# Three edits around the modulation rows of a two-layer S5 and attention trunk

## The chip, the cores and the metric

The kernel runs on one core of one Trainium2 chip. The metric is the device time of one execution in microseconds (us), the median of three runs; smaller is better. A core has a matrix engine (PE, with its weight loads listed apart as PEld), VectorE (DVE), ScalarE (ACT), GpSimd (POOL) and SyncE (SP), each with an instruction stream of its own, which wait for each other on semaphores. DMAs are issued from the streams of SP and ACT here.

## The reference, cut to what matters

Everything is fp32. The sequence has 512 positions of 1024 features, batch 1.

```python
cond = silu(c)
for i in range(2):
    mod = cond @ ada_w[i] + ada_b[i]                    # (1, 6 * 1024)
    sh_t, sc_t, g_t, sh_c, sc_c, g_c = split(mod, 6)
    h = rms_norm(x, norm_g[i, 0]) * (1 + sc_t) + sh_t
    h = s5_mixer(h, ...) if i == 0 else diff_attention(h, ...)
    x = x + g_t * rms_norm(h, norm_g[i, 1])
    h = rms_norm(x, norm_g[i, 2]) * (1 + sc_c) + sh_c
    h = conv_ffn(h, w_in[i], conv_w[i], conv_b[i], w_out[i])
    x = x + g_c * rms_norm(h, norm_g[i, 3])
```

`s5_mixer` ends in a gated product (GLU) with a 1024 x 2048 matrix. `conv_ffn` is an up projection (1024 x 5632), a causal convolution of width 3 along the sequence, `gelu(a) * b`, and a down projection (2816 x 1024).

## The kernel before, in words

All large products run in "units" of weights of 128 x 2048 fp32 (1 MB). SP loads unit `n` into `raw[:, n % 2]`, ACT copies it rounded into `whi` (`split_high`, L783), DVE writes the remainder into `wlo` (`split_low`, L1388), and PE multiplies: each step is three matmuls (hi x hi, lo x hi, hi x lo), 48 matmuls in a unit. One half (slot) of `raw`, `whi` and `wlo` is filled while PE works from the other. SP loads unit `n` once unit `n - 2` has been split (`load_unit`). The stages are the S5 front (Toeplitz tiles `toep`, loaded by 32 DMAs of SP from `kx`, one set of eight for each of four pieces), 8 GLU units, `barrier(0)` (root mean squares, and the hidden input of the next product, made feature tile by feature tile in `next_input` on DVE and `high` on ACT), 22 up units and 12 down units of the first FFN, attention, and a second FFN of the same form.

The modulation of layer 0 and 1 is 2 x 48 x 128 numbers, worked out in six "thirds" of 2048. Each third arises as four rows of 512 in one PSUM bank, on partitions 0, 32, 64 and 96. For layer 0 (thirds 0 to 2) PE makes the rows itself in the S5 front (`ada_unit`, L1867). For layer 1 (thirds 3 to 5) DVE adds up products in `ada_acc` (`ada_step`, L1453), and PE sums over the partitions (`sum_acc`, L1885, eight matmul records). ACT copies the bank into `sq` (`copy_row`, L721; `copy_sums`, L935), and PE turns it by eight matmul records against columns of the identity (`turn_row`, L1879) into 16 columns of bank 7. There DVE reads it in `modulation` (L1307 on) and adds the bias into `modt`.

In the order of the streams: `turn_row(1)` and `turn_row(2)` stand between GLU unit 0 (L2077) and GLU unit 1 (L2043 on). In the first FFN PE runs `sum_acc(0)` after up unit 1, `turn_row(3)` and `sum_acc(1)` after unit 9, `turn_row(4)` and `sum_acc(2)` after unit 13, `turn_row(5)` after unit 15. `barrier(0)` makes `row_of(5)` (L2155) when POOL's first root is there, four idle products (L2116), `row_of(7)` when POOL's second root is there, six idle products, and then the up units begin on the first `hhi` tile (L2051).

For an up unit, ACT's `body` copies the two banks with the last tap into `ca` and `cb` (L925), splits the unit after next (L783), applies gelu (L929), and after POOL's product (L609) writes `ghi` (L931); DVE's `body` does the other taps (L1584, L1588) and then `split_low`; POOL writes `glo` (L611). Down unit 0 has only half the work (24 matmuls), since the first half of its rows is padding; its weights are split in the body of up unit 20, those of down unit 1 in the body of up unit 21, the last.

On ACT `copy_row(1)` stands among the scaling of the S5 input (`scaled`, L740), and `copy_row(2)` just after it, ahead of `z_steps` (L790), `zt_steps` (L800) and the split of the first GLU unit.

Of the kernel before, what the change touches and what calls it, by code (L numbers as in the profile page):

```python
# [24 lines left out]
P = 128  # L25
# [51 lines left out]
def build(nc, a, out_rows):  # L77

    ctx = ExitStack()
    with ctx:  # L80
# [129 lines left out]
        psum = ctx.enter_context(nc.psum_tensor("psum", [P, 8, 512], F32))  # L210

# [40 lines left out]
        acc_psum = sem("acc_psum")  # L252
        turned_x, rows_out = sem("turned_x"), sem("rows_out")
# [418 lines left out]
        def _(act):  # L672
# [49 lines left out]

            def copy_inputs(g, beside=None):

                for n in range(4):
                    act.wait_ge(inb_psum, 4 * g + n + 1)
                    gp = PO * g + 4 * (n % 2)
                    A((inb_im if n // 2 else inb_re)[:, gp:gp + 4, :],
                      psum[:, n % 2, :].rearrange("p (g k) -> p g k", g=4), ACT.Copy).then_inc(inb_ready, 1)
                    if beside:  # L730
                        beside(n)
# [32 lines left out]
            copy_row(1)  # L764
            scaled(1, 3)
# [36 lines left out]

            copy_row(2)
            z_steps(0)
            z_steps(1)
            zt_steps(0)
            act.wait_ge(in_psum, 2)
# [66 lines left out]
            def copy_gate_row(hf, bank):  # L874

                act.wait_ge(mod_psum, 6 + hf)
                A(gate_row[:, SEQ * hf:SEQ * hf + SEQ], psum[:, bank, :], ACT.Copy).then_inc(row_copied, 1)
# [28 lines left out]

            def high(r):

                layer, c0 = shift_col(r)
                for f in range(KT):  # L910
                    act.wait_ge(t_ready, KT * r + f + 1)
                    A(hhi[:, f, :], psum[:, 4 + 2 * (f % 2), :], ACT.Identity,
                      bias=modt[:, layer, c0 + f:c0 + f + 1]).then_inc(h_hi, 1)
                    if r == 2 and f == 1:
                        copy_gate_row(1, 3)

            def ffn(layer):
                n0, g0 = U_FIN[layer], layer * JT

                def body(j, s, half):  # L920
# [6 lines left out]
                    split_high(j + (n0 + 2), s, half + n0 // 2 + 1)  # L927
# [5 lines left out]
                def copy_sums(third):  # L933
                    act.wait_ge(acc_psum, third - 2)
                    A(sq[:, third % 2, :], psum[:, 6, :], ACT.Copy).then_inc(row_copied, 1)  # L935

                body(0, 0, 0)
                body(1, 1, 0)
                if layer == 0:
                    copy_sums(3)  # L940
                    pairs(act, 2, 10, body)
                    copy_sums(4)
                    pairs(act, 10, 14, body)
                    copy_sums(5)
                    pairs(act, 14, JT, body)
                else:
                    pairs(act, 2, JT, body)
# [19 lines left out]
            second_half_high()  # L967
            high(0)
# [154 lines left out]
        def _(dve):  # L1123
# [179 lines left out]
            def modulation(layer, chunks):  # L1303

                for ch in chunks:
                    c = slice(KT * ch, KT * ch + KT)
                    link(TT(modt[:, layer, c], psum[:, 7, 48 * layer + KT * ch:48 * layer + KT * ch + KT],  # L1307
                            ada_b[:, layer, c], ALU.add))
# [269 lines left out]
            def ffn(layer):  # L1578
                n0, g0 = U_FIN[layer], layer * JT

                def body(j, s, half, first=None, second=None):
# [10 lines left out]
                    split_low(j + (n0 + 2), s, half)  # L1592
# [3 lines left out]
                if layer == 0:  # L1596
# [9 lines left out]
                    pairs(dve, 12, 16, body)  # L1606
                    dve.wait_ge(mod_psum, 5)
# [4 lines left out]
                    pairs(dve, 16, JT, body)  # L1612
                else:
                    pairs(dve, 0, JT, body)
# [48 lines left out]
            def glu(i, s):  # L1663
# [193 lines left out]
        def _(pe):  # L1857
# [16 lines left out]
            def turn_row(third):  # L1874

                pe.wait_ge(row_copied, third + 1)
                for q in range(4):
                    out = psum[:, 7, THIRD * third:THIRD * third + THIRD].rearrange("p (b q) -> p q b", q=4)
# [3 lines left out]
            def sum_acc(third, slot):  # L1882

                for b in range(4):
                    ins = M(psum[32 * b:32 * b + 1, 6, :], ones[:, 0:1], ada_acc[:, slot, 512 * b:512 * b + 512],  # L1885
# [38 lines left out]
            turn_row(0)  # L1924
# [175 lines left out]
            turn_row(1)  # L2100
            turn_row(2)
# [57 lines left out]
            def barrier(r):  # L2159
# [30 lines left out]
                if r == 2:  # L2190
                    broadcast_gate(0, 2)
                else:
# [53 lines left out]
            def ffn(layer):  # L2246
# [348 lines left out]
```

## Time and profile before

| | |
|---|---|
| median of three runs (lowest, highest) | 1226.2 us (1224.52, 1226.31) |
| profiled execution, its time and its span | 1226.44 us, 1224.6 us |
| PE busy | 1191.5 us, 97% |
| DVE, ACT, POOL busy | 739.4, 519.1, 398.6 us |
| mean granted clock of PE, as a share of full speed | 0.996 |
| DMA packets, all queues | 26696 |

A row of the profile gives the start or count, the length and the line of `kernel.py`; "idle before" is the time its engine had nothing to do, with the engine that released it. Matmul records overlap: back to back the up units' matmuls are 0.39 us long each and start 0.23 us apart.

### The profile page before, as it was taken

To read this page: it belongs to the slowest core of one execution; us is meant where nothing else is said; L and a number is where in the kernel's file an instruction comes from. 1 tells how busy PE (TensorE), PEld (TensorE's weight loads), DVE (VectorE), ACT (ScalarE), POOL (GpSimd) and SP (SyncE) were. 2 spreads that over 40 slices of the span, in tenths; PEclk is the share of its full clock that TensorE was granted. 3 is DMA by queue.
4 is the path that set the end of the run, shared out by engine and by line. 5 is a ranking of instruction groups with operands and counts; after the bars stand their busy time and mean duration, and the time that the engine had idled before them with its cause. 6 is when DMAs were issued, how large, how long until landed. Compare 5 with 4: busy or idle time off the path is not lost.

```text
span 1224.6 us, 17448 instructions
## 1 busy us (share of the span) xinstructions
PE 1191.5 (97%) x6420; PEld 955.5 (78%) x6420; DVE 739.4 (60%) x979; ACT 519.1 (42%) x791; POOL 398.6 (33%) x272
## 2 busy tenths in 40 slices
PE   6998999999999999999999999999999999999998
PEld 2757888788888887888787777677788888878887
DVE  8999587889864544151963778857744444442323
ACT  4374443444434433132333677755444433442311
POOL 5963200365653342000303354411443344330000
PEclk9999999999999999999999999999999999999999
DMA  9878555157732222232233223202222222223221
GB/s 365 324 270 195 209 206 205 71 210 270 274 110 96 103 103 104 103 105 102 82 104 104 86 70 103 86 35 69 82 95 99 103 103 103 77 94 138 80 92 70
DMA packets 26696, 162.19 MB, mean 132 GB/s; under 512 B 4496, under 2 KB 4816, under 8 KB 8400
## 3 DMA queue, kind: packets, MB, share of 16 engines
q1 hardware_dynamic: 25632, 161.15, 37.5%
q8 instruction: 37, 0.61, 0.2%
q10 hardware_dynamic: 1008, 0.28, 0.1%
q14 instruction: 19, 0.16, 0.0%
HBM read 152.76 MB, written 2.10 MB: 126 GB/s over the span
## 4 chain that ended last, share of the span: by engine, by line
PE 87%; DVE 5%; issue 2%; ACT 2%; POOL 1%; DMA 1%; SPq 1%; DVEq 0%; POOLq 0%; ACTq 0%
PE psum L2043 17%; PE psum L2044 17%; PE psum L2045 17%; PE psum L2307 3%; PE psum L2308 3%; PE psum L2309 3%; PE psum L2207 3%; PE psum L2208 3%; PE psum L2209 3%; PE psum L1906 2%; PE psum L1867 2%; PE psum L2368 1%; PE psum L2389 1%; PE psum L2356 1%; PE psum L2077 1%
## 5 line engine op out<-in xcount | busy, mean ns | idle before, releaser
L2043 PE MATMUL psum<-hhi,whi 128*128 128x512 f32 x896 | 352.2, 393 | 0.5 <-DVE wlo L1388 0.5
L2045 PE MATMUL psum<-hhi,wlo 128*128 128x512 f32 x896 | 349.0, 389 | 0.0
L2044 PE MATMUL psum<-hlo,whi 128*128 128x512 f32 x896 | 348.9, 389 | 0.0
L1388 DVE TENSOR_TENSOR wlo<-raw,whi 128x2048 fp32r<-128x2048 f32 x79 | 186.8, 2364 | 174.6 <-ACT whi L783 174.6
L783 ACT ACTIVATE whi<-raw 128x2048 fp32r<-128x2048 f32 x80 | 153.2, 1915 | 164.4 <-PE psum L2309 76.4
L609 POOL TENSOR_TENSOR ca<-ca,cb 128x512 f32<-128x512 f32 x44 | 143.8, 3268 | 230.5 <-ACT ca L929 230.5
L2043 PEld LDWEIGHTS psum<-hhi,whi 128*128 128x128 f32 x896 | 168.6, 188 | 38.6 <-issue 2.1
L2045 PEld LDWEIGHTS psum<-hhi,wlo 128*128 128x128 f32 x896 | 168.2, 188 | 35.6
L2044 PEld LDWEIGHTS psum<-hlo,whi 128*128 128x128 f32 x896 | 168.3, 188 | 33.4
L1584 DVE SCALAR_TENSOR_TENSOR ca<-psum,convp,ca 128x511 f32<-128x511 f32 x44 | 33.0, 749 | 200.4 <-ACT ca L925 200.4
L931 ACT ACTIVATE ghi<-ca 128x512 f32 (+1 forms) x44 | 27.8, 632 | 156.6 <-POOL ca L609 156.6
L925 ACT ACTIVATE ca<-psum,convp 128x512 f32<-128x512 f32 x44 | 34.2, 778 | 120.3 <-PE psum L2045 112.7
L599 POOL TENSOR_TENSOR stat<-nwt,power 128x4 f32<-128x4 f32 x6 | 6.4, 1069 | 227.0 <-DVE nwt L1515 223.1
L611 POOL TENSOR_TENSOR glo<-ca,ghi 128x512 f32 (+1 forms) x44 | 66.8, 1517 | 41.3 <-ACT ghi L931 41.3
L2207 PE MATMUL psum<-whi,ghi 128*128 128x512 f32 x176 | 68.9, 391 | 0.8 <-DVE wlo L1388 0.8
L2307 PE MATMUL psum<-ghi,whi 128*128 128x512 f32 x176 | 68.6, 390 | 0.7 <-DVE wlo L1388 0.7
L2209 PE MATMUL psum<-whi,glo 128*128 128x512 f32 x176 | 68.5, 389 | 0.0
L2308 PE MATMUL psum<-glo,whi 128*128 128x512 f32 x176 | 68.5, 389 | 0.0
L2208 PE MATMUL psum<-wlo,ghi 128*128 128x512 f32 x176 | 68.5, 389 | 0.0
L2309 PE MATMUL psum<-ghi,wlo 128*128 128x512 f32 x176 | 68.5, 389 | 0.0
L1453 DVE SCALAR_TENSOR_TENSOR ada_acc<-ada_ring,cond,ada_acc 128x2048 f32<-128x2048 f32 x24 | 62.4, 2600 | 0.0
L1017 ACT ACTIVATE prob<-psum,stat 128x128 f32<-128x128 f32 (+3 forms) x64 | 33.1, 523 | 18.0 <-DVE stat L1726 17.7
(404 smaller groups left out, 1890.6 us busy)
## 6 DMA issues: line engine op xcount, KB each, us to landing
raw<-in_units SPq DMA_DIRECT2D x92, 1024.0 KB, 4.8
ada_raw<-in_ada_w SPq DMA_DIRECT2D x24, 1024.0 KB, 6.9
ada_ring<-in_ada_w SPq DMA_DIRECT2D x24, 1024.0 KB, 4.8
qk_sw<-ca SPq DMA_DIRECT2D x32, 128.0 KB, 2.3
u<-in_x_blocks SPq DMA_DIRECT2D x1, 2048.0 KB, 9.7
x<-in_x_t SPq DMA_DIRECT2D x1, 2048.0 KB, 9.6
out_rows<-y_late SPq DMA_DIRECT2D x8, 256.0 KB, 2.1
bc_par<-in_s_bc SPq DMA_DIRECT2D x1, 1024.0 KB, 5.1
```

The source lines that it names most:

```text
L609: nc.gpsimd.tensor_tensor(ca[:, s, :], ca[:, s, :], cb[:, s, :], ALU.mult).then_inc(g_ready, 1)
L783: A(whi[:, s, :], raw[:, s, :], ACT.Copy).then_inc(split_hi, 1)
L1388: TT(wlo[:, s, :], raw[:, s, :], whi[:, s, :].bitcast(F32), ALU.subtract).then_inc(split_lo, 1)
L2043: M(out, w_hi, hi[:, k, :], start=(k == 0), stop=False)
L2044: M(out, w_hi, lo[:, k, :], start=False, stop=False)
L2045: return M(out, w_lo, hi[:, k, :], start=False, stop=(k == KT - 1))
L2207: M(out, ghi[:, row, tok], whi[:, s, w], start=(isinstance(v, int) and row == 0), stop=False)
L2208: M(out, ghi[:, row, tok], wlo[:, s, w], start=False, stop=False)
L2209: return M(out, glo[:, row, tok], whi[:, s, w], start=False, stop=(isinstance(v, int) and row == JT - 1))
L2307: M(out, whi[:, s, w], ghi[:, row, :], start=(fixed and row == 0), stop=False)
L2308: M(out, whi[:, s, w], glo[:, row, :], start=False, stop=False)
L2309: return M(out, wlo[:, s, w], ghi[:, row, :], start=False, stop=(fixed and row == JT - 1))
```

## The change

1. The turning of thirds 1, 2, 4 and 5 leaves PE. After the copy into `sq`, ACT waits for its own copy and stores the four rows in a DRAM tensor `mod_rows` (`store_row`), and somewhat later loads them back turned, 128 partitions of 16 numbers (`load_row`). In DRAM neighbouring numbers of a partition lie 128 numbers apart. DVE waits for `row_landed` in place of `mod_psum`, and adds the bias to `modt` in place.
2. `sum_acc(0)` and `turn_row(3)` move into `barrier(0)`: the sum takes the place of the four idle products between the two roots, the turn that of four of the six idle products after the second. Both use PSUM bank 3. ACT copies the sum ahead of `high(0)` and, after the second tile of `high(0)`, copies the turned columns into `modt`; PE waits for that (`row_read`) before the second half of up unit 1, which writes bank 3.
3. In both layers the body of the last up unit splits its unit of weights (down unit 1) ahead of the taps, on ACT and on DVE.
4. DVE computes layer 1's modulation after up unit 17, not 15. Some loops are cut at other places for this.

```diff
+        mod_rows = nc.dram_tensor("mod_rows", (4, THIRD, P), F32, kind="Internal").ap()
+            def store_row(third, n):
+                act.wait_ge(row_copied, third + 1)
+                act.dma_start(mod_rows[n].rearrange("(b q) m -> b (q m)", b=4),
+                              sq[0:P:32, third % 2, :]).then_inc(row_stored, 16)
+            def load_row(third, n):
+                act.wait_ge(row_stored, 16 * (n + 2))
+                act.dma_start(modt[:, third // 3, THIRD * (third % 3):THIRD * (third % 3) + THIRD],
+                              mod_rows[n].rearrange("c m -> m c"),
+                              allow_slow_non_contiguous=True).then_inc(row_landed, 16)
...
             for quarter in range(3):
                 scaled(1, quarter)
             copy_row(1)
+            store_row(1, 0)
             scaled(1, 3)
...
+            load_row(1, 0)
             copy_row(2)
+            store_row(2, 1)
             z_steps(0)
             z_steps(1)
             zt_steps(0)
+            load_row(2, 1)
             act.wait_ge(in_psum, 2)
             split_high(0, 0, 0)
...
+                    if r == 0 and f == 1:
+                        act.wait_ge(mod_psum, 1)
+                        A(modt[:, 1, 0:THIRD], psum[:, 3, 0:THIRD], ACT.Copy).then_inc(row_read, 1)
...
-                def body(j, s, half):
+                def body(j, s, half, split_first=False):
+                    if split_first:
+                        split_high(j + (n0 + 2), s, half + n0 // 2 + 1)
                     act.wait_ge(unit_done, j + (n0 + 1))
...
                 if layer == 0:
-                    copy_sums(3)
                     pairs(act, 2, 10, body)
-                    copy_sums(4)
-                    pairs(act, 10, 14, body)
-                    copy_sums(5)
-                    pairs(act, 14, JT, body)
+                    copy_sums(4, 6)
+                    store_row(4, 2)
+                    pairs(act, 10, 12, body)
+                    load_row(4, 2)
+                    pairs(act, 12, 14, body)
+                    copy_sums(5, 6)
+                    store_row(5, 3)
+                    pairs(act, 14, 16, body)
+                    load_row(5, 3)
+                    pairs(act, 16, JT - 2, body)
                 else:
-                    pairs(act, 2, JT, body)
+                    pairs(act, 2, JT - 2, body)
+                body(JT - 2, 0, JT // 2 - 1)
+                body(JT - 1, 1, JT // 2 - 1, split_first=True)
...
             second_half_high()
+            copy_sums(3, 3)
             high(0)
... DVE
-                    pairs(dve, 12, 16, body)
-                    dve.wait_ge(mod_psum, 5)
+                    pairs(dve, 12, 18, body)
+                    dve.wait_ge(row_landed, 16 * 5)
+                    dve.wait_ge(row_read, 2)
                     modulation(1, range(6))
...
-                    dve.wait_ge(mod_psum, 2)
+                    dve.wait_ge(row_landed, 16 * 3)
                     modulation(0, (2, 3, 4, 5))
... PE, GLU and barrier(0)
-            turn_row(1)
-            turn_row(2)
             glu(1, 1, 0)
...
+                elif r == 0:
+                    pe.wait_ge(ada_added, KT)
+                    sum_acc(0, 3)
                 else:
                     idle_products(4, 0)
                 pe.wait_ge(r2_ready, r + 1)
...
+                elif r == 0:
+                    turn_row(3, 3)
+                    idle_products(2, 0)
                 else:
                     idle_products(6, 0)
... PE, first FFN
+                else:
+                    pe.wait_ge(row_read, 2)
                 for k in range(KT):
                     ins = gemm_step(1, KT + k, hhi, hlo)
                 ins.then_inc(unit_done, 1)
                 if layer == 0:
-                    pe.wait_ge(ada_added, KT)
+                    pairs(pe, 2, 10, body)
                     pe.wait_ge(row_clear, 2)
-                    sum_acc(0, 0)
-                    pairs(pe, 2, 10, body)
-                    turn_row(3)
                     pe.wait_ge(ada_added, 2 * KT + 3)
-                    sum_acc(1, 1)
+                    sum_acc(1, 6)
                     pairs(pe, 10, 14, body)
-                    turn_row(4)
+                    pe.wait_ge(row_copied, 5)
                     pe.wait_ge(ada_added, 3 * KT)
-                    sum_acc(2, 0)
-                    pairs(pe, 14, 16, body)
-                    turn_row(5)
-                    pairs(pe, 16, JT, body)
+                    sum_acc(0, 6)
+                    pairs(pe, 14, JT, body)
```

## Rows read from the trace of the kernel before

**Rows 1.** The page's first part: busy time, share of the span and instructions of PE.

```profile
PE 1191.5 (97%) x6420; PEld 955.5 (78%) x6420; DVE 739.4 (60%) x979; ACT 519.1 (42%) x791; POOL 398.6 (33%) x272
```

**Rows 2.** Waits of PE over the span: total, times, longest us; the one on a DMA.

```profile
PE psum L1960 <- DMA toep<-kx: 3.1, 1, 3.1
```

**Rows 3.** Timeline around GLU unit 0's end: start, length, idle before.

```profile
133.39 1.84 PE L1879 MATMUL psum<-ident,sq 128*128 128x4 f32 x16
...
135.09 0.49 PE L2043 MATMUL psum<-hhi,whi 128*128 128x512 f32 x1
```

**Rows 4.** Timeline around the sum after up unit 1.

```profile
242.76 2.28 DVE L1388 TENSOR_TENSOR wlo<-raw,whi 128x2048 fp32r<-128x2048 f32 x1
...
244.31 0.39 PE L2045 MATMUL psum<-hhi,wlo 128*128 128x512 f32 x1
...
244.63 1.04 PE L1885 MATMUL psum<-ada_acc,ones 128*1 128x512 f32 x8
...
245.60 0.50 PE L2043 MATMUL psum<-hhi,whi 128*128 128x512 f32 x1
```

**Rows 5.** The chain that ended last, after up unit 9: start, us.

```profile
332.93 0.79 PE psum L1879 x8
```

**Rows 6.** Timeline around the turn after up unit 15.

```profile
402.01 0.95 PE L1879 MATMUL psum<-ident,sq 128*128 128x4 f32 x8
...
402.82 0.49 PE L2043 MATMUL psum<-hhi,whi 128*128 128x512 f32 x1
```

**Rows 7.** Timeline of the step from up to down, layer 0, then layer 1.

```profile
468.65 0.78 ACT L925 ACTIVATE ca<-psum,convp 128x512 f32<-128x512 f32 x1 [3.04 <-PE psum L2045]
...
470.00 1.92 ACT L783 ACTIVATE whi<-raw 128x2048 fp32r<-128x2048 f32 x1
...
472.23 2.28 DVE L1388 TENSOR_TENSOR wlo<-raw,whi 128x2048 fp32r<-128x2048 f32 x1
...
473.46 0.39 PE L2309 MATMUL psum<-ghi,wlo 128*128 128x512 f32 x1
...
474.57 0.50 PE L2307 MATMUL psum<-ghi,whi 128*128 128x512 f32 x1 [0.72 <-DVE wlo L1388]
...
1101.81 0.50 PE L2207 MATMUL psum<-whi,ghi 128*128 128x512 f32 x1 [0.80 <-DVE wlo L1388]
```

**Rows 8.** POOL's product of layer 0's last up unit, then ACT's next split.

```profile
472.59 3.06 POOL L609 TENSOR_TENSOR ca<-ca,cb 128x512 f32<-128x512 f32 x1 [5.50 <-ACT ca L929]
...
476.32 1.90 ACT L783 ACTIVATE whi<-raw 128x2048 fp32r<-128x2048 f32 x1
```

**Rows 9.** PE's timeline in barrier 0, from the first root on.

```profile
217.57 1.17 PE L2116 MATMUL psum<-whi 128*128 128x512 f32 x4
218.91 1.16 PE L2155 MATMUL psum<-ident,stat 128*128 128x128 f32 x8 [0.18 <-POOL stat L599]
219.82 1.63 PE L2116 MATMUL psum<-whi 128*128 128x512 f32 x6
221.73 0.47 PE L2051 MATMUL psum<-hhi,whi 128*128 128x512 f32 x1 [0.27 <-ACT hhi L912]
```

**Rows 10.** ACT's third row copy in the S5 front.

```profile
93.00 0.60 ACT L721 ACTIVATE sq<-psum 128x512 f32<-128x512 f32 x1 [3.27 <-PE psum L1867]
```

**Rows 11.** SP's issues of the Toeplitz DMAs: duration ns min/median/max.

```profile
L325 SPq DMA_DIRECT2D toep<-kx x32: 583/591/1797, 83.2 to 109.0; - x32
```

**Rows 12.** The chain that ended last, in the S5 front.

```profile
108.96 4.38 DMA toep<-kx
...
113.38 3.51 PE psum L1960 x32
```

**Rows 13.** Windows of the S5 front; the third value from the end is PE's clock.

```profile
114.00:116.00 2.00, 2.00 (x24) 2.00 (x21) 1.07 (x2) 0.00 (x0) 0.76 (x1) 0.50 0.54 209
```

**Rows 14.** DMA queues (q1 SP's, q10 ACT's): packets, MB, share of 16 engines.

```profile
q1 hardware_dynamic: 25632, 161.15, 37.5%
...
q10 hardware_dynamic: 1008, 0.28, 0.1%
```

More of the change, by code:

```diff
@@ L252, in build @@
         acc_psum = sem("acc_psum")
+        row_stored, row_landed, row_read = cond_in, bc_in, uab_ready
         turned_x, rows_out = sem("turned_x"), sem("rows_out")
@@ L874, in copy_gate_row @@
             def copy_gate_row(hf, bank):
-                act.wait_ge(mod_psum, 6 + hf)
+                act.wait_ge(mod_psum, 2 + hf)
                 A(gate_row[:, SEQ * hf:SEQ * hf + SEQ], psum[:, bank, :], ACT.Copy).then_inc(row_copied, 1)
@@ L905, in copy_rows, with copy_sums @@
                 A(ac_rows[:], psum[:, 6, :], ACT.Copy).then_inc(ac_copied, 1)
+            def copy_sums(third, bank):
+                act.wait_ge(acc_psum, third - 2)
+                A(sq[:, third % 2, :], psum[:, bank, :], ACT.Copy).then_inc(row_copied, 1)
             def high(r):
@@ L926, in body @@
                           scale=convp[:, layer, j, i, 2:3], bias=convp[:, layer, j, i, 3:4]).then_inc(tap2, 1)
-                    split_high(j + (n0 + 2), s, half + n0 // 2 + 1)
+                    if not split_first:
+                        split_high(j + (n0 + 2), s, half + n0 // 2 + 1)
                     act.wait_ge(conv_done, 2 * j + (2 * g0 + 1))
@@ L931, in body @@
                     A(ghi[:, j, :], ca[:, s, :], ACT.Copy).then_inc(g_hi, 1)
-                def copy_sums(third):
-                    act.wait_ge(acc_psum, third - 2)
-                    A(sq[:, third % 2, :], psum[:, 6, :], ACT.Copy).then_inc(row_copied, 1)
                 body(0, 0, 0)
@@ L1306, in modulation @@
                     c = slice(KT * ch, KT * ch + KT)
-                    link(TT(modt[:, layer, c], psum[:, 7, 48 * layer + KT * ch:48 * layer + KT * ch + KT],
-                            ada_b[:, layer, c], ALU.add))
+                    row = psum[:, 7, c] if layer == 0 and ch < 2 else modt[:, layer, c]
+                    link(TT(modt[:, layer, c], row, ada_b[:, layer, c], ALU.add))
                 for ch in chunks:
@@ L1579, in ffn, with body @@
                 n0, g0 = U_FIN[layer], layer * JT
-                def body(j, s, half, first=None, second=None):
+                def body(j, s, half, first=None, second=None, split_first=False):
+                    if split_first:
+                        split_low(j + (n0 + 2), s, half)
                     for i, dst in enumerate((ca, cb)):
@@ L1591, in body @@
                         first(j, s, half)
-                    split_low(j + (n0 + 2), s, half)
+                    if not split_first:
+                        split_low(j + (n0 + 2), s, half)
                     if second:
@@ L1611, in ffn @@
                     signal(mod_ready)
-                    pairs(dve, 16, JT, body)
+                    pairs(dve, 18, JT - 2, body)
                 else:
-                    pairs(dve, 0, JT, body)
+                    pairs(dve, 0, JT - 2, body)
+                body(JT - 2, 0, JT // 2 - 1)
+                body(JT - 1, 1, JT // 2 - 1, split_first=True)
                 r, m0 = 2 * layer + 1, U_FOUT[layer]
@@ L1872, in _, with turn_row, sum_acc @@
             bx = on[:].rearrange("p t s -> p (t s)")
-            def turn_row(third):
+            def turn_row(third, bank):
                 pe.wait_ge(row_copied, third + 1)
                 for q in range(4):
-                    out = psum[:, 7, THIRD * third:THIRD * third + THIRD].rearrange("p (b q) -> p q b", q=4)
+                    out = psum[:, bank, 0:THIRD].rearrange("p (b q) -> p q b", q=4)
                     ins = M(out[:, q], sq[:, third % 2, P * q:P * q + P], ident[:, 0:P:32], start=True, stop=True)
                 ins.then_inc(mod_psum if third else mod0_psum, 1)
-            def sum_acc(third, slot):
+            def sum_acc(slot, bank):
                 for b in range(4):
-                    ins = M(psum[32 * b:32 * b + 1, 6, :], ones[:, 0:1], ada_acc[:, slot, 512 * b:512 * b + 512],
+                    ins = M(psum[32 * b:32 * b + 1, bank, :], ones[:, 0:1], ada_acc[:, slot, 512 * b:512 * b + 512],
                             start=True, stop=True)
@@ L1923, in _ @@
             pe.wait_ge(u_normed, OCTS)
-            turn_row(0)
+            turn_row(0, 7)
             ada_units(KT, 11)
```

## The prediction

> **What bounds the kernel now.** I read the page's busy times first: PE is busy for 1191.5 of 1224.6 us, and no other engine passes 60% [rows 1]. So a microsecond comes off only where PE itself does less, or where it stands still; the second kind is 33 us in all. The waits of PE name one that matters here: 3.1 us in the S5 front, on a Toeplitz DMA [rows 2]. The rest stands in barriers, attention and at two steps from up to down. After that I went through the timelines around each place that the diff touches.
>
> Two readings come back below. Back to back, matmuls of the large products start 0.23 us apart though each is 0.39 us long. The first one after another kind of work is 0.49 to 0.50 long and the next follows 0.1 us late, so a change of kind costs 0.1 us beyond its own time.
>
> **Turns 1 and 2 leave the GLU.** The sixteen records begin in the slot that a GLU matmul would have had, at 133.39, and the GLU goes on at 135.09 [rows 3]: 1.70 us, with the late start 1.80. Nothing else holds GLU unit 1: its weights and its banks are long there. Later in the GLU every engine's work hangs on PE's unit ends, with idle time in each unit on ACT and DVE, so the gain is handed on to barrier 0. Gain 1.80.
>
> **The sum after up unit 1 leaves the FFN.** Without it PE would go on 0.23 us after the start at 244.31, at 244.54. But the weights of unit 2 are ready only when DVE's split ends, 242.76 + 2.28 = 245.04, and PE starts some 0.06 us after such an end, at 245.10, in place of 245.60 [rows 4]. Of the sum's 0.97 us only 0.50 comes back; 0.56 becomes a wait on `wlo`. Gain 0.50.
>
> **Turns 3, 4 and 5 leave the FFN.** Turn 3 costs 0.79 [rows 5], and turn 4 the same after unit 13; a sum stays beside each, so the 0.1 us of a change of kind stays: 1.58 together. Turn 5 stands alone: 402.82 - 402.01 = 0.81, and 0.1 with it, 0.91 [rows 6]. The splits of the units that follow are ready over 1 us before PE wants them, so no wait shows up. Gain 2.49.
>
> **The last up unit's split goes first.** In layer 0 ACT is released at 468.65 by the end of the last up unit, does both taps and splits at 470.00; DVE's split starts at 472.23 and ends at 474.51. PE has done down unit 0 by 473.46 + 0.23 = 473.69 and starts at 474.57 [rows 7]: 0.88 late, and 0.11 for the restart, 0.99. With the split first, ACT ends it at 468.65 + 1.92 = 470.57, and DVE at about 470.6 + 2.28 = 472.9, 0.8 us before PE asks. In layer 1 the idle time is 0.80 where layer 0 shows 0.72 [rows 7], so 1.07. What is late next is the last convolution. DVE's taps would begin near 472.9, not 469.6, and POOL's product near 475.6, not 472.59; ACT's next split moves with it from 476.32 to about 479.3 [rows 8], and DVE's ends by 479.3 + 1.9 + 2.3 = 483.5. PE wants it after the 48 matmuls of down unit 1, at 473.69 + 10.9 = 484.6. There is 1.1 us left, so no new wait. Gain 2.06.
>
> **What barrier 0 takes in.** PE is done with the first `row_of` at 217.57 and gets the second root at 218.91 [rows 9], 1.34 us later. The sum needs 0.97 to 1.04 [rows 4] and ends by about 218.7. ACT's copy of it, 0.60 by the like copy [rows 10], ends near 219.4, before PE is through `row_of` at 219.82. The turn (0.79) and two idle products end near 221.1, and the first up matmul waits for `hhi` until 221.73 anyway [rows 9]. ACT's small copy out of bank 3 falls where it waits for the third tile, and `row_read` comes some 15 us before its use. I cost all of this at nothing. If the sum came out longer than 1.34 us, each tenth over it would be on the path.
>
> **The new DMAs.** The two issues of a third stand on ACT's queue. An issue of SP's, of a pattern with many runs, takes 0.59 us in the median [rows 11]. Behind `store_row(1, 0)` are ACT's scalings, which run 2.7 us ahead of the next thing that they would hold up; `load_row(1, 0)` and `store_row(2, 1)` stand beside a wait of 3.27 us [rows 10]; `load_row(2, 1)` delays the split of GLU unit 0, wanted 15 us later. In the FFN ACT stands idle for 3 us in each unit [rows 7]. All are covered as long as an issue takes under about 3 us. The landings are wanted late too: layer 0's at 141, 34 us after the last issue, layer 1's two units after it.
>
> What is not covered is the transfer itself. Each `load_row` moves 2048 numbers of 4 bytes that don't lie together in DRAM, and the two of layer 0 fall at about 90 and 106 us. There SP issues the last two Toeplitz pieces one behind the other, and PE waits for the last: issued at 108.96, landed after 4.38 us, and only then do the 32 matmuls run [rows 12]. Any delay of SP's issues or of that landing is on the path whole. The trace of before has no such transfer. From below the price is nothing: a queue of its own, and gaps between SP's transfers. From above, ACT's queue shows 1008 packets at 0.1%, which is under 0.15% of 16 x 1224.6 us, or 29 us, so under 29 ns each [rows 14]; 2048 over 16 engines are 3.7 us, and two loads 7.5, if SP's DMAs stood still meanwhile. SP's own issues show what a busy DMA side does: 0.59 in the median, 1.80 at most [rows 11]. I take one more such slow issue or as much in the landing, 1.80 - 0.59 = 1.2 us, as the transfers overlap others' gaps for the most part.
>
> The Trainium skill ("DMA: Bandwidth & Descriptors", "Rules for kernel authors") says that a last dimension that isn't contiguous becomes one descriptor per element; no row of before can show that, and q10's count after will. Its "Queues, rings and completion order" has an engine alternate between queues by whole packets of some 9 to 17 descriptors. By that rule each of the roughly three turns of the last piece on an engine waits behind up to 17 elements, which at 29 ns is 3 x 0.5 = 1.5 us in place of 1.2, and the sum would be 5.35 instead of 5.65.
>
> **Sum.** 1.80 + 0.50 + 2.49 + 2.06 = 6.85, less 1.2, is 5.65. The profiled execution took 1226.44 us, its span 1224.6 and 1.84 around it; 1226.44 - 5.65 = 1220.8. The median of the runs is 0.24 lower, so I say 1220.5.
>
> **Rivals.**
> (a) The loads cost nothing in the front: 1226.2 - 6.85 = 1219.35. For it: a separate queue and few bytes. Against: the piece's landing is the one DMA that PE waits for.
> (b) The loads cost 3 to 9 us in the front, through longer issues of SP or a later landing, and also because PE's longer rest then lengthens the half-clock stretch seen at 114 to 116 [rows 13]. At 5 us: 1224.4.
> (c) Slower than before: an element costs as much as an average packet of SP's queue, 37.5% of 16 x 1224.6 us over 25632, or 287 ns [rows 14]. A Toeplitz piece is 576 runs of 1 KB, 36 per engine; if each of the last piece's waits behind one element, that is 10.3 us, and 1226.2 - 6.85 + 10.3 = 1229.7. It decides from about 9.3 us of delay, or 260 ns an element. Against it: the 29 ns of ACT's own queue.
> (d) The clock drops in barrier 0, where turns with four columns replace idle products of 512. The 32 matmuls after the stop in the front took 3.51 us with PE granted half its clock, 1.2 GHz [rows 12, 13], so 1.8 us are lost there: 1222.3.
> (e) The step from up to down keeps its wait, since the split is held by something else (the landing of `raw`, or ACT coming late): 1222.6.
>
> **Chances.** My forecast (a delay of 0.5 to 3 us) 0.42, (a) 0.28, (b) 0.12, (c) 0.06, (d) 0.07, (e) 0.05. A measurement of this kernel tells about 0.2%, 2.45 us, from no change. Below 1223.75 lie my case, (a), (d), (e) and a little of (b): 0.82. Within lie most of (b): 0.11. Slower is (c) with a rest for what I did not see: 0.07. The range goes from 1218.0, which is (a) less the 1.3 us by which runs differ and a little, to 1225.3, which is (b) at 6 us.
>
> **What would show it.** PE's L1879 falls from 48 records to 16, with none between 133 and 135 nor after 300; the sum leaves 244 and a PE wait of about 0.5 on `wlo` appears there; the waits of L2307 and L2207 on `wlo` vanish; `q10` rises from 1008 packets to some 9300 if every number is a packet; the wait for `toep` at L1960 grows from 3.1 by the front's price. GLU unit 1 should start 1.7 us earlier relative to the end of unit 0. I would be wrong if that wait grew by over 4 us, if L2051 started later relative to the roots, or if a split with the taps behind it made down unit 2 wait.

## The result and the profile after

| | before | after |
|---|---|---|
| median of six runs (lowest, highest), us | 1224.07 (1222.76, 1226.31) | 1218.33 (1216.53, 1219.82) |
| profiled execution: time, span, us | 1226.44, 1224.6 | 1216.53, 1214.7 |

The ratio is 0.995, 95% interval 0.9938 to 0.9961: 6.1 us faster (4.8 to 7.6), against a forecast of 5.65. The changed kernel's median lies in the predicted range of 1218.0 to 1225.3 but only 0.3 us above its lower end (two of the six runs are below it), and 2.2 us below the predicted 1220.5. Of these 2.1 are the level of the kernel before, whose median had been 1226.2 over three runs and was 1224.07 over six. One execution of the kernel of experiment 3 took 1990 us at a granted clock of 0.56, where all others are near 1.0; it is left out everywhere.

The two profiled executions differ by 9.9 us, more than the medians do: one stands at the upper end of its kernel's runs, the other at the lower. So totals of the two profiles can't be subtracted. What can be compared is each stage by itself.

The page of the kernel after, parts 1 and 3 (busy time; DMA queues with packets, MB and share of 16 engines):

```profile
PE 1183.2 (97%) x6380; PEld 947.8 (78%) x6380; DVE 741.2 (61%) x979; ACT 519.4 (43%) x792; POOL 394.0 (32%) x272
...
q1 hardware_dynamic: 25632, 161.15, 37.4%
q10 hardware_dynamic: 9296, 0.34, 0.6%
```

PE does 40 records less than in [rows 1]: 32 of the four turns, and 8 idle products of barrier 0. The 16 records of turns that are left are those of thirds 0 and 3. `q10` [rows 14] went from 1008 packets to 9296: 4 loads of 2048 numbers are 8192, a packet for each number (what the other 96 are isn't shown); the forecast was some 9300. The Trainium skill ("DMA: Bandwidth & Descriptors", "Rules for kernel authors") gives one descriptor per element for such a pattern, and the count agrees.

Waits of PE in the kernel after (total, times, longest), the two that bear on the change:

```profile
PE psum L2000 <- DMA toep<-kx: 2.5, 2, 1.4
...
PE psum L2083 <- DVE wlo L1422: 0.9, 2, 0.5
```

The wait for `toep` (L1960 before, L2000 after) is 2.5 where [rows 2] has 3.1. But these are two waits: 1.1 us at 93.5 for an earlier piece, which the first profile of before doesn't have, and 1.4 us for the last piece, where it has 3.1. The earlier one says nothing on the loads: other profiles have it or not (0 to 1.2 us), with and without loads there. The new wait on `wlo` is there, at up unit 2 of layer 0 (0.4 us); the other one in this row, 0.5 us in layer 1, was there before. The waits of the first down matmuls on `wlo`, 0.72 and 0.80 in [rows 7], are gone.

The second view is the timeline of barrier 0, PE and then ACT (L2193 was L2155, L1925 is the sum, L1919 the turn, L2154 the idle products, L2091 the first up matmul):

```profile
213.01 1.06 PE L2193 MATMUL psum<-ident,stat 128*128 128x128 f32 x8
214.00 1.04 PE L1925 MATMUL psum<-ada_acc,ones 128*1 128x512 f32 x8
215.17 1.16 PE L2193 MATMUL psum<-ident,stat 128*128 128x128 f32 x8
216.16 0.95 PE L1919 MATMUL psum<-ident,sq 128*128 128x4 f32 x8
216.97 0.71 PE L2154 MATMUL psum<-whi 128*128 128x512 f32 x2
217.99 0.47 PE L2091 MATMUL psum<-hhi,whi 128*128 128x512 f32 x1 [0.30 <-ACT hhi L936]
```

```profile
215.10 0.60 ACT L929 ACTIVATE sq<-psum 128x512 f32<-128x512 f32 x1 [1.67 <-PE psum L1925]
...
219.12 0.18 ACT L942 ACTIVATE modt<-psum 128x16 f32<-128x16 f32 x1
```

From the first `row_of` of the second root to the first up matmul it is 217.99 - 215.17 = 2.82 us, as before: 221.73 - 218.91 = 2.82 [rows 9]. The sum fits between the two roots, and the turn and two idle products end before `hhi` comes. Barrier 0 takes both at no cost.

The step from up to down in layer 0, timelines of ACT, DVE, POOL and PE in turn (L799 and L1422 are the splits, L954 is ACT's tap, L1620 DVE's, L611 POOL's product, L2348 the first matmul of down unit 0):

```profile
461.75 1.92 ACT L799 ACTIVATE whi<-raw 128x2048 fp32r<-128x2048 f32 x1 [3.39 <-PE psum L2085]
463.57 0.76 ACT L954 ACTIVATE ca<-psum,convp 128x512 f32<-128x512 f32 x1
...
470.66 1.90 ACT L799 ACTIVATE whi<-raw 128x2048 fp32r<-128x2048 f32 x1
```

```profile
463.70 2.29 DVE L1422 TENSOR_TENSOR wlo<-raw,whi 128x2048 fp32r<-128x2048 f32 x1 [7.15 <-ACT whi L799]
465.90 0.74 DVE L1620 SCALAR_TENSOR_TENSOR ca<-psum,convp,ca 128x511 f32<-128x511 f32 x1
```

```profile
468.80 1.29 POOL L611 TENSOR_TENSOR ca<-ca,cb 128x512 f32<-128x512 f32 x1 [8.96 <-ACT ca L959]
```

```profile
461.49 0.39 PE L2348 MATMUL psum<-ghi,whi 128*128 128x512 f32 x1
```

The split of down unit 1 is done at 465.99, 4.5 us after down unit 0 began at 461.49; down unit 0 alone is 5.5 us long (24 matmuls, 0.23 apart), so PE finds it ready. The next split of ACT comes at 470.66, which is 9.2 us after the first matmul of down unit 0, where before it was 476.32 - 468.25 = 8.1 us ([rows 8], and the first matmul below).

```profile
468.25 0.39 PE L2307 MATMUL psum<-ghi,whi 128*128 128x512 f32 x1
```

### The profile page after: what moved, and what is told of

Same layout as the page of the kernel before. It is cut to its first block, busy times and chain, and to the rows that moved or that the text cites. A ratio compares the mean times of both kernels' runs of the same rounds, so it can differ in the third digit from the quotient of the medians.

```text
span 1214.7 us, 17258 instructions
## 1 busy us (share of the span) xinstructions
PE 1183.2 (97%) x6380; PEld 947.8 (78%) x6380; DVE 741.2 (61%) x979; ACT 519.4 (43%) x792; POOL 394.0 (32%) x272
## 3 DMA queue, kind: packets, MB, share of 16 engines
q10 hardware_dynamic: 9296, 0.34, 0.6%
## 4 chain that ended last, share of the span: by engine, by line
PE 87%; DVE 6%; issue 2%; ACT 1%; POOL 1%; DMA 1%; SPq 1%; DVEq 0%; POOLq 0%; ACTq 0%
PE psum L2083 17%; PE psum L2085 17%; PE psum L2084 17%; PE psum L2350 3%; PE psum L2349 3%; PE psum L2348 3%; PE psum L2251 3%; PE psum L2252 3%; PE psum L2253 3%; PE psum L1946 2%; PE psum L1907 2%; PE psum L2409 1%; PE psum L2430 1%; PE psum L2397 1%; PE psum L2117 1%
## 5 line engine op out<-in xcount | busy, mean ns | idle before, releaser
L1422 DVE TENSOR_TENSOR wlo<-raw,whi 128x2048 fp32r<-128x2048 f32 x79 | 187.9, 2378 | 185.1 <-ACT whi L799 185.1
L799 ACT ACTIVATE whi<-raw 128x2048 fp32r<-128x2048 f32 x80 | 153.2, 1915 | 166.9 <-PE psum L2350 74.3
L611 POOL TENSOR_TENSOR ca<-ca,cb 128x512 f32<-128x512 f32 x44 | 137.6, 3128 | 235.6 <-ACT ca L959 235.6
L1620 DVE SCALAR_TENSOR_TENSOR ca<-psum,convp,ca 128x511 f32<-128x511 f32 x44 | 32.9, 748 | 182.6 <-ACT ca L954 182.6
L954 ACT ACTIVATE ca<-psum,convp 128x512 f32<-128x512 f32 x44 | 34.2, 778 | 114.0 <-PE psum L2085 106.4
L2348 PE MATMUL psum<-ghi,whi 128*128 128x512 f32 x176 | 68.5, 389 | 0.0
```

What stands on the lines that cost most here:

```text
L611: nc.gpsimd.tensor_tensor(ca[:, s, :], ca[:, s, :], cb[:, s, :], ALU.mult).then_inc(g_ready, 1)
L799: A(whi[:, s, :], raw[:, s, :], ACT.Copy).then_inc(split_hi, 1)
L1422: TT(wlo[:, s, :], raw[:, s, :], whi[:, s, :].bitcast(F32), ALU.subtract).then_inc(split_lo, 1)
L2348: M(out, whi[:, s, w], ghi[:, row, :], start=(fixed and row == 0), stop=False)
```

## Where the time came from, stage by stage

The table has the distances between the first matmuls of consecutive stages, us, from the profiles of the kernels below and of the two kernels themselves (each of which was profiled twice; the profile of "after, second" is that of experiment 5, that of "before, second" is that of experiment 10). The fifth column runs from the first matmul of down unit 0 of layer 1 to that of the last part of the down projection:

| kernel | GLU unit 0 to 1 | GLU unit 1 to up unit 0 | up unit 0 to down unit 0 | down unit 0 to attention | layer 1, last down part | start of GLU unit 0 |
|---|---|---|---|---|---|---|
| before | 13.6 | 86.6 | 246.5 | 129.8 | 107.2 | 121.5 |
| before, second | 13.6 | 86.6 | 246.5 | 129.8 | 107.2 | 118.5 |
| after | 11.9 | 86.5 | 243.5 | 128.7 | 106.1 | 119.6 |
| after, second | 11.9 | 86.5 | 243.5 | 128.7 | 106.1 | 119.5 |
| edit 3 alone | 13.7 | 86.6 | 246.6 | 128.7 | 106.1 | 120.5 |
| turns 1, 2 on PE | 13.6 | 86.6 | 243.5 | 128.7 | 106.1 | 118.7 |
| third 3 in the FFN | 11.9 | 86.5 | 244.8 | 128.7 | 106.1 | 121.2 |
| loads late | 11.9 | 86.5 | 243.5 | 128.7 | 106.1 | 122.5 |
| loads late, second | 11.9 | 86.5 | 243.5 | 128.7 | 106.1 | 118.4 |

Five of the six columns repeat to 0.1 us. They give 1.7 + 0.15 + 3.0 + 1.05 + 1.1 = 7.0 us, where the prediction had 1.80 + 2.99 + 0.99 + 1.07 = 6.85. The 0.15 of the second column, 86.64 to 86.49, belongs to turns 1 and 2: with them on PE again it is 86.6. Inside the third column the sums of the layer-1 thirds are marks that both kernels have. From up unit 0 to the sum after unit 9 it is 1.28 us less, from there to the sum after unit 13 0.78 less, and from there to down unit 0 0.96 less; to up unit 2 alone it is 23.37 in place of 23.87. So the sum gave 0.50, turn 3 0.78, turn 4 0.78 and turn 5 0.96.

The sixth column, the front, wanders over 4 us, in both kernels and with loads or without. One stretch that the table leaves out wanders too: attention and the up projection of layer 1, from attention's first matmul to down unit 0 of layer 1, take 496.0 to 497.5 us in these profiles (497.4 and 496.0 before, 496.4 and 497.5 after).

## The experiments

All are compared with runs of the kernel before on the same chip: experiments 1 to 4 on one chip, 5 to 8 on a second, 9 and 10 on a third. Medians in us; the ratio is to that kernel.

**1. Edit 3 alone.** The kernel before, with the last up unit's split ahead of its taps and nothing else of the change. ACT's part of the edit is shown; DVE's is alike.

```diff
+                    if split_first:
+                        split_high(j + (n0 + 2), s, half + n0 // 2 + 1)
                     act.wait_ge(unit_done, j + (n0 + 1))
```

> The kernel before with edit 3 alone (the last up unit's split first, both layers). My sum: 0.99 + 1.07 = 2.06 us less than before; PE's two waits on wlo at the steps from up to down vanish and no wait appears at down unit 2. Rival (the wait moves to down unit 2, or the step is held by the landing of raw): 0 to 1 us less.

Measured: 1222.24 against 1224.65, ratio 0.9981 (0.9969 to 0.9992), 2.3 us faster. The two stages behind the up units are 1.1 us shorter each, all others unchanged. PE's waits on `wlo` at both steps are gone and none took their place, so the split was what held them, and rival (e) falls.

**2. Turns 1 and 2 on PE again**, all else as in the changed kernel.

```diff
-            store_row(1, 0)
...
-            load_row(1, 0)
...
+            turn_row(1, 7, THIRD)
+            turn_row(2, 7, 2 * THIRD)
             glu(1, 1, 0)
```

> The changed kernel with thirds 1 and 2 turned on PE again between GLU units 0 and 1, so without layer 0's stores and loads. Theory 1 (the sum stands, and the loads cost about 1.1 us in the S5 front on average): 5.05 us less than before, 0.7 more than the changed kernel; the GLU has its 1.8 us back. Rival (the loads cost nothing in the front, and another term of the sum gives 1.1 us less): 3.9 less than before.

Measured: 1217.89 against 1224.65, ratio 0.9952 (0.9933 to 0.997), 5.9 us faster. GLU unit 0 to 1 is 13.6 us again and GLU unit 1 to up unit 0 86.6, so the 1.85 us of this part are real. The times don't show them: the median is as that of the changed kernel over its twelve runs (1217.78), the mean, 1218.47, is 0.6 above theirs (1217.85), and the forecast was 0.7 more. Taken as they are, the times leave 1.2 us (means) to 1.7 (medians) for what layer 0's stores and loads cost in the front; but these are seven runs that spread over 5 us, partly on another chip. The rival's 3.9 us less lies in the interval too; it is the stage table that speaks against it.

**3. Both layer-0 row loads late**, behind the last `zt_steps`, when every Toeplitz piece has landed.

```diff
-            load_row(1, 0)
...
-            load_row(2, 1)
...
             zt_steps(3)
+            load_row(1, 0)
+            load_row(2, 1)
```

> The changed kernel with both row loads of layer 0 issued after the last zt_steps, behind the Toeplitz DMAs, some 14 us before DVE wants them. Theory 1 (the loads delay SP's issues and the last piece's landing): the front's cost of about 1.1 us comes back, 6.8 less than before. Rival: no difference to the changed kernel, 5.7 less than before. If the landing takes over 14 us, DVE's modulation is late and the GLU lengthens.

Measured: 1216.59 against 1224.65, ratio 0.9934 (0.9918 to 0.9951), 8.1 us faster (6.0 to 10.0), where theory 1 had 6.8 and the rival 5.7. It was run again in experiment 6, beside the changed kernel.

**4. The first up unit's split ahead of its taps too**, on top of the changed kernel, in both layers, on ACT (shown) and on DVE. If the split gates the first down unit it gates up unit 2 as well, where the new wait on `wlo` is.

```diff
-                body(0, 0, 0)
+                body(0, 0, 0, split_first=True)
```

> The changed kernel with up unit 0's split (for unit 2) ahead of its taps too, in both layers. In the changed kernel PE waits for wlo twice, 0.5 us each, at unit 2. If the order of the split is what holds it, both waits go: 2 x 0.6 = 1.2 us less than the changed kernel, 6.9 less than before. Rival: DVE is full there (its product for ada_acc takes 3.4 us beside POOL), so unit 1's taps come late and a later unit waits: 0 to 0.5 us.

Measured: 1219.67 against 1224.65, ratio 0.996 (0.9947 to 0.9973): 4.9 us faster than before, but slower than the changed kernel. The expectation was wrong. The waits of PE in this kernel, and PE's first matmul of unit 2 (here L2086):

```profile
PE psum L2086 <- DVE cb L1624: 3.3, 2, 1.7
```

```profile
244.33 0.49 PE L2086 MATMUL psum<-hhi,whi 128*128 128x512 f32 x1 [1.67 <-DVE cb L1624]
```

Unit 2 writes the two banks that unit 0's taps read, so it needs the taps as well as the split. The wait went from `wlo` (0.45 each) to the taps (1.65 each), 1.3 us more in layer 0 and 1.1 in layer 1: up unit 0 to down unit 0 is 244.8 in place of 243.5. At the last up unit the order pays because no up unit comes after it that wants those banks.

**5. The changed kernel again.** 

> The changed kernel, unaltered, once more, so that its mean and its front can be compared with the others on one chip. Theory 1 (a fixed gain of 6.8 us in the stages behind the front, and a front whose length varies by chance and with PE's clock): -5.5 to -7 us against before; of the stages, GLU unit 0 to 1, FFN 0 and FFN 1 repeat to within 0.2 us what the first profile showed (11.9, 243.5, 106.1), while the front's start of GLU unit 0 lies anywhere from 118.7 to 122.5. Rival (the two row loads lengthen the front by 1.2 us): the start of GLU unit 0 is later here than in the kernel with late loads, and the time is higher by some 1.2 us.

Measured: 1217.37 against 1225.67, ratio 0.9937 (0.992 to 0.9953), 7.7 us faster. Its stages repeat the first profile's to 0.1 us, and GLU unit 0 starts at 119.5; with late loads it started at 122.5 and 118.4.

**6. Late loads again, beside it.** 

> Both layer-0 row loads after the last zt_steps, behind all Toeplitz pieces, once more, now beside the changed kernel on one chip. Theory 1 (the loads cost at most 0.5 us in the front): 0 to 0.5 us below the changed kernel. Rival, as forecast (the loads cost 1.2 us in the front): 1.2 us below it. The last Toeplitz piece lands at 112 to 113.5 by both.

Measured: 1216.57 against 1225.67, ratio 0.9935 (0.9918 to 0.9952). The median is 0.8 us below the changed kernel's; the ratios are alike. This lies between the two theories, and the intervals are too wide to tell 0.4 from 1.2 us.

**7. Each layer-0 row load four times.** The three extra ones go to a scratch tile, and DVE's counts of landed rows are raised to match.

```diff
+                if n < 2:
+                    for i in range(3):
+                        act.dma_start(modx[:, 3 * n + i, :], mod_rows[n].rearrange("c m -> m c"),
+                                      allow_slow_non_contiguous=True).then_inc(row_landed, 16)
```

> The changed kernel with each of the two layer-0 row loads issued four times (the three extra ones into a scratch tile); it amplifies the price of the transfers by four, 6144 packets more in each place. Theory 1 (the loads cost the front nothing to 0.3 us): at most 1 us above the changed kernel, apart from ACT's own issues, 6 x 0.38 us, which are covered. Rival, as forecast (1.2 us for the pair): 3 x 1.2 = 3.6 us above it, and the last Toeplitz piece lands 3 us or more later (about 116), or SP's issues of it grow. If packets cost as the rival with 29 ns on every engine has it, a load keeps 16 engines busy for 3.7 us and the six extra ones for 22 us, which would show as a landing at over 118.

Measured: 1224.05 against 1225.67, ratio 1.0 (0.9981 to 1.0018): 6.7 us above the changed kernel on the same chip. Neither theory had that. The timeline of ACT in this kernel, and of PE (L735 is the row load, L740 the extra ones, L804 the split, L2005 the products with the last Toeplitz piece, L2031 the next ones):

```profile
105.38 0.38 ACTq L735 DMA_DIRECT2D modt<-mod_rows  x1
...
105.78 2.05 ACTq L740 DMA_DIRECT2D modx<-mod_rows  x1
...
107.86 8.00 ACTq L740 DMA_DIRECT2D modx<-mod_rows  x2
115.96 1.91 ACT L804 ACTIVATE whi<-raw 128x2048 fp32r<-128x2048 f32 x1 [7.73 <-issue]
```

```profile
114.14 1.97 PE L2005 MATMUL psum<-toep,u 128*64 128x128 f32 x32 [2.48 <-DMA toep<-kx]
120.74 1.54 PE L2031 MATMUL psum<-ident,z 128*128 128x128 f32 x6 [4.63 <-ACT z L811]
```

The extra issues, one behind another, take 2.0 to 5.1 us each, where a single one takes 0.38, and ACT works at nothing meanwhile: PE waits 4.6 us for ACT's `z`. That is most of the 6.7 us, and it is a price of ACT's issues, not of the Toeplitz piece. Behind PE's longer rest another 1.4 us is lost: from this start on `z` to GLU unit 0 it takes 6.04 us where the changed kernel takes 4.66, and the granted clock falls to 0.57 in the windows 120 to 122 and 122 to 124.

The piece itself gives the price asked for: PE starts on it at 114.14, where the kernels with one load each start at 112.9 to 113.0 (four profiles). 1.1 us for three more pairs of loads is 0.4 us a pair. SP's last issue comes early here, at 107.93, so the landing itself took 6.2 us, against 3.8 to 5.5 (mean 4.5) with one load each; by that it is 0.6 a pair. This is one profile, and landings differ by as much as this between others, so 0.4 to 0.6 is an estimate. The packets were not 29 ns each either: the page of this kernel gives `q10` 21680 packets at 1.2% of 16 x 1221.8 us, or 11 ns a packet.

```profile
q10 hardware_dynamic: 21680, 0.39, 1.2%
```

**8. Late loads, and two products of 512 columns ahead of the last Toeplitz wait**, in the time in which PE rests.

```diff
             def local(piece, first=True, filled=0):
+                if filled:
+                    wait(pe, z_ready, 2 * (piece - 1))
+                    for _ in range(filled):
+                        M(psum[:, 4, :], ident[:], toep[2]..., start=True, stop=True)
```

> The kernel with late loads, and before PE waits for the last Toeplitz piece it does two products whose result nobody reads (128x512, fp32, into a bank that is free). Theory 1 (the 1.5 us by which the 32 matmuls behind that wait take 3.5 instead of 2.0 us come from PE's rest ahead of them, after which the granted clock is 0.50): the 32 matmuls take 2.0 us in the profile, the rest before them shrinks by the length of the two products, and the median is up to 1.5 us below the kernel with late loads, with less spread. Rival (the half clock has another cause, or the added products run into the piece's landing): 0 to 1 us above it, the 32 matmuls 3.5 us long.

Measured: 1216.98 against 1225.67, ratio 0.993 (0.9915 to 0.9945); with late loads alone it is 1216.57. No gain. The timeline of PE (L1998 are the added products):

```profile
111.17 1.88 PE L1998 MATMUL psum<-toep,ident 128*128 128x512 f32 x4
113.50 1.97 PE L2005 MATMUL psum<-toep,u 128*64 128x128 f32 x32 [0.45 <-DMA toep<-kx]
```

The 32 products keep the full clock, as they did in six other profiles without such filling, and the granted clock over the run is 0.9995 in the mean of six, against 0.9986 with late loads alone. But the added products end at 113.05, and in other profiles the piece is there from 111.9 on: what they save in one execution they can cost in the next. This stays inconclusive on the cause.

**9. Third 3 back in the FFN.** Sum after up unit 1 and turn after unit 9 as before, idle products in barrier 0; the rest as changed.

```diff
-                elif r == 0:
-                    pe.wait_ge(ada_added, KT)
-                    sum_acc(0, 3)
...
-                elif r == 0:
-                    turn_row(3, 3)
-                    idle_products(2, 0)
...
+                    pe.wait_ge(ada_added, KT)
+                    pe.wait_ge(row_clear, 2)
+                    sum_acc(0, 6)
                     pairs(pe, 2, 10, body)
-                    pe.wait_ge(row_clear, 2)
+                    turn_row(3, 7)
```

> The changed kernel with third 3 back in the FFN: the sum after up unit 1, its turn after unit 9, both on PE, and idle products in barrier 0 again; thirds 1, 2, 4 and 5 still go through device memory and the last units still split first. Theory 1 (the sum gave back 0.50, since 0.56 of it became a wait on wlo, the turn 0.79, and barrier 0 took both at no cost): up unit 0 to down unit 0 takes 243.5 + 0.50 + 0.79 = 244.8 us, GLU unit 1 to up unit 0 stays at 86.5, and the median is 1.3 us above the changed kernel. Rival (PE gets the sum's whole 0.97 back, and the barrier paid a part): the stretch takes 245.3 or more, while GLU unit 1 to up unit 0 becomes shorter by 0.3 us or more.

Measured: 1218.85 against 1225.99, ratio 0.9946 (0.993 to 0.9962); 1.1 us above the changed kernel's median over its twelve runs, 1217.78, of which six at least were on another chip. Up unit 0 to down unit 0 takes 244.8, the expected number, and barrier 0's stage stays at 86.5. The chain of this kernel shows the sum with no wait around it (first fence), where in the changed kernel the timeline shows the wait that took its place (second):

```profile
242.37 0.23 PE psum L2084
242.60 0.97 PE psum L1924 x8
243.57 0.43 PE psum L2082
```

```profile
239.03 2.28 DVE L1422 TENSOR_TENSOR wlo<-raw,whi 128x2048 fp32r<-128x2048 f32 x1
...
241.36 0.50 PE L2083 MATMUL psum<-hhi,whi 128*128 128x512 f32 x1 [0.40 <-DVE wlo L1422]
```

So half of what the sum cost came back and the rest is a wait for the split, as the prediction had it.

**10. The kernel before again.** 

> The kernel before, unaltered, for a second profile. Theory 1 (what differs between single executions is the front and a stretch at the end of attention, through PE's granted clock): GLU unit 0 to 1, up unit 0 to down unit 0, and the last down units repeat to 0.1 us (13.6, 246.5, 107.2), while the start of GLU unit 0 lies anywhere from 118.7 to 122.5 and the wo product takes 67.7 or 69.1. Rival (the first profile's 1226.44 is what this kernel costs): all of them repeat, with 121.5 and 69.1.

Measured: one execution, 1222.06 us, span 1220.3, granted clock 1.0: 4.4 us below the profiled execution on which the prediction's sum stood. The chain of its front, and a window (third value from the end: PE's clock):

```profile
107.87 4.04 DMA toep<-kx
...
111.96 1.97 PE psum L1960 x32
```

```profile
114.00:116.00 2.00, 2.00 (x28) 1.83 (x29) 1.97 (x4) 1.01 (x3) 0.65 (x1) 1.00 0.07 29
```

Against [rows 12, 13] the piece comes 1.4 us earlier and the 32 products take 1.97 at full clock, not 3.51 at half, which is 1.5 us. The other 1.4 of the 4.4 us lie between attention and down unit 0 of layer 1 (496.0 in place of 497.4), where the first profile of before has a second such stretch; the windows of that profile and of this one:

```profile
784.00:792.00 8.00, 5.91 (x21) 4.01 (x20) 7.58 (x13) 5.52 (x12) 4.18 (x4) 0.81 0.15 37
```

```profile
780.00:788.00 8.00, 5.75 (x26) 4.03 (x27) 7.59 (x13) 5.31 (x12) 4.98 (x4) 1.00 0.08 13
```

The other stages repeat to 0.1 us, as theory 1 had it.

## What the front and the clock do to a single execution

Each run lists PE's mean granted clock. Grouped by it, over all 49 runs of the kernel before that list it, 12 of the changed kernel and 11 with late loads (mean time in us, and how many runs):

| granted clock | before | after | after, loads late |
|---|---|---|---|
| 1.000 | 1222.94 (10) | none | 1215.95 (3) |
| 0.999 | 1223.41 (10) | 1216.65 (5) | 1215.79 (3) |
| 0.998 | 1225.11 (11) | 1218.48 (5) | 1217.39 (3) |
| 0.997 | 1226.43 (4) | 1219.30 (2) | 1219.26 (2) |
| 0.996 | 1226.60 (14) | none | none |

At the same clock the change is worth 6.8, 6.6 and 7.1 us. That is the 7.0 us of the stages less at most a few tenths for the loads, though groups of two to five runs can't place a tenth. With late loads it is 7.0 to 7.7. Over 0.004 of granted clock the time of before differs by 3.7 us, and the profile behind the prediction was one at 0.996: two half-clock stretches cost it 1.5 and some 1.4 us. The grouping shows that the two go together. It doesn't show that the clock alone makes the difference, since 1.4 us of the 4.4 between the two profiles of before are a piece that landed earlier.

## Why the prediction was right or wrong

The stages went as forecast, 7.0 us against 6.85. Two terms of the sum had the wrong size: the level from which the gain was taken, 1226.2 where six runs give 1224.07, and the 1.2 us for layer 0's loads, of which the last piece's landing shows 0.4 to 0.6.

- **Turns 1 and 2: 1.80.** Measured 1.7 in GLU unit 0 to 1 and 0.15 behind it, 1.85; right, by experiment 2 and the stage table.
- **Sum after up unit 1: 0.50, with a new wait of 0.56 on `wlo`.** Right: the stretch to up unit 2 is 0.50 shorter, the stage moved by 1.3, the expected 0.5 + 0.8, when third 3 was put back (experiment 9), and the wait is there (0.40 on PE's record).
- **Turns 3, 4, 5: 2.49.** Measured 0.78 + 0.78 + 0.96 = 2.52. Only turn 3 was put back by itself; turns 4 and 5 are read from the distances in the two profiles.
- **Last up unit's split first: 2.06.** Right: 2.1 in the stages, 2.3 (1.0 to 3.8) as a kernel by itself. "What is late next" was too dark: POOL's product took 1.29 us, not 3.06 [rows 8], where DVE had stopped by then, and ACT's next split moved back by 1.1 us, not by 3.
- **Barrier 0 at nothing.** Right, 2.82 us on both sides; rival (d) didn't occur. Its price of 1.8 us, half of 3.51, was too high also: the same 32 products take 1.97 at full clock, so 1.5 are lost.
- **Less 1.2 us for the layer-0 loads.** This term of the sum was mis-sized, as far as the landing shows. By it a pair costs 0.4 to 0.6 us (experiment 7). The kernels without loads there (seven profiles, among them both of before) start on the piece at 111.9 to 113.5, mean 112.6, and those with them at 112.9 to 113.0: 0.4 again, inside the spread. Late against early loads comes out at 0.8 us in the medians of one chip and 0.95 in the means of all runs, and experiment 2 leaves 1.2 or more, so 1.2 can't be excluded by times; what the loads cost in the mean of many executions stays open. The estimate of the prediction by alternating queues (the Trainium skill, "DMA: Bandwidth & Descriptors", "Queues, rings and completion order") came to 1.5 us with 29 ns an element, which was only an upper bound; with the 11 ns of experiment 7 the same working gives an estimate of 0.6. No run here shows the alternation itself. SP's issues beside the loads were 1.38 and 1.19 us against 1.62 and 1.80 before: long issues come with or without them.
- **The level: "the median of the runs is 0.24 lower, so I say 1220.5".** This is the step that failed most: it makes 2.1 of the 2.2 us by which the forecast missed. Three runs of 1224.5 to 1226.3 and a profile of 1226.44 were taken for the kernel's level. Over 49 runs it goes from 1222 to 1228 with a median of 1225.03 (so the six runs of the result lie low in their turn, by 1.0), and the profile contained two half-clock stretches that cost some 1.5 us each, of which [rows 12, 13] show the first, and a late piece. With 6.85 - 0.4 off the six-run median of 1224.07 the forecast would have been 1217.6, against 1218.33 and, in the second set, 1217.37.
- **Rivals.** (a), loads free, is nearest in the time, and by the landing the truth lies between it and the forecast. (b), (c) and (e) fall, (c) by the 11 ns an element against its 260; (b)'s mechanism of long issues exists, but on ACT's queue and only when loads follow each other (experiment 7).

The best version measured is the changed kernel with late loads, 1216.57 to 1216.59 in two sets, 8.0 us under the kernel before; its lead over the changed kernel is 0.8 us in the medians of one chip and not certain.

## What to carry to other kernels

When the bound engine stands still for a known while at a barrier, small work of its own placed there is free if it is shorter than the gap between the two releases; the whole barrier is not the measure. Taking an instruction off the bound engine gives back only what lies behind the next operand's arrival; read when that operand is ready before counting the gain. Before putting a split ahead of other work of the same engine, list everything that the next product needs of that engine: ahead of the taps it helped only where the next product didn't want the banks that the taps read.

And where the gain is half a per cent, take the level from many runs and compare stages, or runs at equal granted clock, not two whole profiles.

## What the hardware showed that was not expected

- Loads of 2048 single numbers: 0.38 us to issue and 4.7 us to land (3.8 to 7.4, four loads) when alone; back to back the later issues take 2.0 to 5.1 us each (median 2.9) and land after 7.8 to 14.1 us (experiment 7). Two late loads in a row show it too: the second issue took 1.5 us in one profile and 4.7 in the other. The issuing engine does nothing else meanwhile (7.73 us idle ahead of ACT's split in experiment 7). Each number is a packet of some 11 ns.
- SP's issue of a Toeplitz DMA takes 0.59 us, but of the last dozen in a front two or three take 0.8 to 1.9, with loads beside them or without (all twelve profiles).
- Whether the 32 products after PE's rest in the front run at 1.2 or 2.4 GHz isn't settled by the length of the rest: after 2.9 us of it they took 1.97 us at full clock in the second profile of the changed kernel, after 1.9 us they took 3.63 at half clock in experiment 9. In the twelve profiles half clock follows five times, after rests of 1.9 to 3.1 us, and full clock seven times, after rests of 0.5 to 2.9. What decides it stays open.
- POOL's 128x512 product took 1.29 us with DVE at rest, 3.06 beside DVE's split [rows 8], and 3.13 in the mean of all 44 in the changed kernel.
